# Decoder step: the merge's stick-breaking products placed between the steps of dilated attention

## What is computed

```python
u = rmsnorm(h);  z = u @ W_in        # q, k, v of 12 dilated and 8 stick-breaking heads, gates ga, gb
oa = combine_groups(dilated_prompt(q, k, v, win, dil, slopes) for 3 dilations)   # 256 features a token
ob = sb_prompt(q, k, v, bias)                                                    # 512 features a token

def merge_out(x, oa, ob, ga, gb, w_oa, w_ob, w_out):
    ya = oa.reshape(*lead, H_G * HEAD_DIM) @ w_oa
    yb = ob.reshape(*lead, B_W) @ w_ob
    return x + (jax.nn.sigmoid(ga) * ya + jax.nn.sigmoid(gb) * yb) @ w_out

h += hier_moe(rmsnorm(h))            # one of 4 groups, then 2 of its 8 experts
h += sigmoid(rmsnorm(h) @ w_pg) * (p @ w_pp)
```

## Time and profile before

| | |
|---|---|
| three runs | 1991.63, 1993.75, 1997.38 us (median 1993.75) |
| the profiled execution | 1992.05 us, its span 1990.4 us |
| PE, DVE, ACT, POOL busy over the span | 88%, 60%, 49%, 10% |

### The profile page before, as it was taken

How to read it: one execution, slowest core, us unless ns; L and a number is a source line. 1 busy time by engine, 2 the same in 40 slices (tenths; PEclk the granted TensorE clock), 3 DMA queues, 4 the chain that set the end, 5 groups by cost and what they waited for, 6 DMA issues and landing times. The chain is left out here.

```text
span 1990.4 us, 27436 instructions
## 1 busy us (share of the span) xinstructions
PE 1752.8 (88%) x9832; PEld 1485.7 (75%) x9832; DVE 1201.3 (60%) x1554; ACT 966.8 (49%) x1360; POOL 195.8 (10%) x304
## 2 busy tenths in 40 slices
PE   4999999979888888676688977999999999997498
PEld 3999999978666666454587855788888888885485
DVE  5111222162589997432564246899999999996485
ACT  4221111111566775134442014677777777775255
POOL 1000111130000000000130012111111111110100
PEclk8999999989999999685899978999999999999699
DMA  5443455363351200601336225999999999994641
GB/s 170 108 133 116 128 173 159 117 203 111 119 160 56 73 33 12 201 2 28 120 113 208 100 86 207 390 376 372 376 379 383 368 386 379 377 372 191 222 150 65
DMA packets 154089, 384.28 MB, mean 193 GB/s; under 512 B 21668, under 2 KB 94996, under 8 KB 133525
## 3 DMA queue, kind: packets, MB, share of 16 engines
q1 hardware_dynamic: 119732, 313.43, 44.1%
q0 software_dynamic: 15424, 36.00, 5.6%
q10 hardware_dynamic: 18848, 33.74, 4.8%
HBM read 331.09 MB, written 76.35 MB: 205 GB/s over the span
## 5 line engine op out<-in xcount | busy, mean ns | idle before, releaser
L96 PE MATMUL p_acc<-uh,p_wl 128*128 128x344 f32 x720 | 234.0, 325 | 10.1 <-DVE ul L414 10.1
L97 PE MATMUL p_acc<-ul,p_wh 128*128 128x344 f32 x720 | 230.5, 320 | 0.0
L98 PE MATMUL p_acc<-uh,p_wh 128*128 128x344 f32 x720 | 230.3, 320 | 0.0
L391 ACT ACTIVATE p_zc<-p_acc 128x344 f32<-128x344 f32 x90 | 41.2, 458 | 290.4 <-PE p_acc L98 281.7
L2452 DVE TENSOR_TENSOR x_wgl<-x_wg,x_wgh 128x2048 fp32r<-128x2048 f32 x66 | 148.4, 2288 | 28.0 <-ACT x_wgh L2389 20.3
L2452 DVE TENSOR_TENSOR x_wul<-x_wu,x_wuh 128x2048 fp32r<-128x2048 f32 x66 | 148.3, 2288 | 18.7 <-ACT x_wuh L2389 18.7
L2474 DVE TENSOR_TENSOR x_wdl<-u,x_wdh 128x1024 fp32r<-128x1024 f32 x128 | 148.2, 1220 | 9.7 <-ACT x_wdh L2395 9.7
L96 PEld LDWEIGHTS p_acc<-uh,p_wl 128*128 128x128 f32 x720 | 135.6, 188 | 13.4 <-issue 8.5
L427 DVE COPY u<-p_tp 128x512 f32<-128x512 f32 x40 | 25.8, 686 | 185.3 <-PE p_tp L344 185.3
L97 PEld LDWEIGHTS p_acc<-ul,p_wh 128*128 128x128 f32 x720 | 135.7, 189 | 0.0
L98 PEld LDWEIGHTS p_acc<-uh,p_wh 128*128 128x128 f32 x720 | 135.7, 189 | 0.0
(11 more groups left out here) (378 smaller groups left out, 4240.5 us busy)
## 6 DMA issues: line engine op xcount, KB each, us to landing
x_wg<-in_w_gate SPq DMA_DIRECT2D x64, 1024.0 KB, 7.9
x_wu<-in_w_up SPq DMA_DIRECT2D x64, 1024.0 KB, 7.6
u<-in_w_down SPq DMA_DIRECT2D x32, 2048.0 KB, 12.3
zT<-p_zc ACTq DMA_DIRECT2D x30, 516.0 KB, 2.7
p_w<-in_w_in SPq DMA_DIRECT2D x30, 512.0 KB, 5.4
ztok<-u POOLq DMA_DIRECT2D x20, 512.0 KB, 4.6
m_gate<-gT SPq DMA_DIRECT2D x16, 516.0 KB, 4.4
f_y<-ys POOLq DMA_DIRECT2D x16, 512.0 KB, 5.2
```

What stands on the lines that cost most here:

```text
L96: pe.matmul(out, w_low, m_high, start=first, stop=False)
L97: pe.matmul(out, w_high, m_low, start=False, stop=False)
L98: return pe.matmul(out, w_high, m_high, start=False, stop=last)
L391: act.activation(zc[:, b, s * NS:(s + 1) * NS], acc[b * NSPLIT + s][:, 0:NS], ACT.Copy).then_inc(zc_full, 1)
```

## The change

The 288 products of `w_ob` with the stick-breaking outputs (8 chunks x 3 pieces x 12) leave `merge` and are issued inside `dilated` by `other_part`, by a table `plan`: 12 in each of the steps 15, 16, 17, 36, 37, 56 and 60, and 6 in each of the steps 18 to 35 and 38 to 53. They sum in one bank `yacc`; ACT evicts each piece (`keep`) to `kept_y` and stores a full chunk to DRAM (`ybT`). ACT cuts the high parts (`boh`, `woh`) and GpSimd the low parts (`bol`, `wol`). To find room, q, k and v hold one pair at a time, and SP loads the second pair's over the first's as they come free; the two value banks become one (`O`), its eviction moves to step lag 20, and DVE's eviction to the front of the step. In `merge` a piece has 6 products; `ybT` comes back by DMA with the gates, and is multiplied from SBUF. The constants of `route` are made by GpSimd during `residual`, and ranks and inverse move to before products 0, 4 and 5. mTh, mTl and `x_idx` get longer rows.

```diff
-        EXP_LAG, TURN_LAG, VALUE_LAG, EVICT_LAG, SUM_LAG, INV_LAG, DONE_LAG = 18, 19, 20, 21, 26, 28, 32
+        EXP_LAG, TURN_LAG, VALUE_LAG, EVICT_LAG, SUM_LAG, INV_LAG, DONE_LAG = 18, 19, 20, 20, 26, 28, 32
...
+        M = 3 * CB
+        PIECES = KD * NSPLIT
+
+        first_p1 = score_step(UNITS)
+        plan = {n: M // 2 for n in range(EXP_LAG, first_p1 + UNITS)}
+        plan.update({n: M // 2 for n in range(first_p1 + EXP_LAG, first_p1 + UNITS + EXP_LAG)})
+        plan.update({n: M for n in (EXP_LAG - 3, EXP_LAG - 2, EXP_LAG - 1, first_p1 + EXP_LAG - 2, first_p1 + EXP_LAG - 1,
+                                    first_p1 + UNITS + VALUE_LAG, last_unit[-1] + SUM_LAG - 1)})
+        first_m, n_m = {}, 0
+        for n in sorted(plan):
+            first_m[n] = n_m
+            n_m += plan[n]
+        evict_at = {n + 1: first_m[n] // M for n in plan if (first_m[n] + plan[n]) % M == 0}
+
+        q = sb("q", [P, N_DIL, SEQ])
+        k = sb("k", [P, N_DIL, SEQ])
+        v = sb("v", [P, N_DIL, QT, P])
+        boh = sb("boh", [P, CB, NT], F32R)
+        bol = sb("bol", [P, CB, NT], F32R)
+        woh = sb("woh", [P, 2, CB, P], F32R)
+        wol = sb("wol", [P, 2, CB, P], F32R)
+        wo = g["m_w"][:, :, 2:2 + CB, :]
+        kept_y = g["spare"]
...
-        O = [ps(f"O{n}", [P, 512]) for n in range(2)]
-        nat_ps = O[0][0:ROWS, P:2 * P]
-        inv_ps = O[0][0:ROWS, 2 * P:3 * P]
-        far_ps = O[0][:, 3 * P:3 * P + ROWS].rearrange("p (b i) -> p b i", b=2)
-        sum_ps = O[0][:, 3 * P + ROWS:3 * P + 2 * ROWS].rearrange("p (b i) -> p b i", b=2)
+        O = ps("O", [P, 512])
+        yacc = ps("yacc", [P, 512])
...
+                    if p_ == 0:
+                        sp.wait_ge(row_full, 2 * QT)
+                        load_qk(sp, 1, 0)
+                    else:
+                        sp.wait_ge(o_full, QT)
+                        load_v(sp, 1, [0])
                     sp.wait_ge(row_full, 2 * (p_ + 1) * UNITS)
                     classes_out(p_, mst, 1, mrows[:, p_, 1, :], m_out[p_][1], m_in[p_][1])
+                    if p_ == 0:
+                        load_qk(sp, 1, 1)
+                        load_qk(sp, 1, 2)
+                    else:
+                        sp.wait_ge(o_full, UNITS)
+                        load_v(sp, 1, [1, 2])
...
+            def weight_low(c):
+                pool.wait_ge(woh_full, c + 1)
+                pool.tensor_tensor(wol[:, c % 2, :, :], wo[:, c % 2, :, :], woh[:, c % 2, :, :], ALU.subtract).then_inc(wol_full, 1)
+
+            for c in range(2):
+                weight_low(c)
+            for kk in range(CB):
+                pool.wait_ge(boh_full, kk + 1)
+                pool.tensor_tensor(bol[:, kk, :], obT[:, kk, :], boh[:, kk, :], ALU.subtract).then_inc(bol_full, 1)
+            for c in range(2, KD):
+                weight_low(c)
...
-                if a >= 2:
-                    evicted(a - 2)
-                if a % 2 == 0:
-                    bank_read(at_step)
+                if a >= 1:
+                    evicted(a - 1)
+                bank_read(at_step)
...
+            def other_part(s):
+                for m in range(first_m[s], first_m[s] + plan[s]):
+                    piece, x = divmod(m, M)
+                    c, t = piece // NSPLIT, slice(piece % NSPLIT * NS, (piece % NSPLIT + 1) * NS)
+                    kk, n = divmod(x, 3)
+                    if x == 0:
+                        pe.wait_ge(wol_full, c + 1)
+                        need(pe, y_full, piece)
+                    if piece == 0 and n == 0:
+                        pe.wait_ge(bol_full, kk + 1)
+                    last = pe.matmul(yacc[:, 0:NS], (wol, woh, woh)[n][:, c % 2, kk, :], (boh, bol, boh)[n][:, kk, t],
+                                     start=(x == 0), stop=(x == M - 1), skip_group_check=True)
+                    if x == M - 1:
+                        last.then_inc(yacc_full, 1)
...
+                if s in plan:
+                    other_part(s)
...
+            def load_weight(c):
+                need(act, wol_full, c - 1)
+                act.dma_start(wo[:, c % 2, :, :], wob[:, :, c * P:(c + 1) * P]).then_inc(wo_in[c % 2], 16)
+
+            def weight_high(c):
+                act.wait_ge(wo_in[c % 2], 16 * (c // 2 + 1))
+                need(act, yacc_full, (c - 1) * NSPLIT)
+                act.activation(woh[:, c % 2, :, :], wo[:, c % 2, :, :], ACT.Copy).then_inc(woh_full, 1)
+
+            def keep(piece):
+                c, n = divmod(piece, NSPLIT)
+                need(act, y_out[c % 2], 16 * (c // 2))
+                act.wait_ge(yacc_full, piece + 1)
+                act.activation(kept_y[:, c % 2, n * NS:(n + 1) * NS], yacc[:, 0:NS], ACT.Copy).then_inc(y_full, 1)
+                if n == 0 and 1 <= c and c + 3 < KD:
+                    load_weight(c + 3)
+                if n == NSPLIT - 1:
+                    if c + 2 < KD:
+                        weight_high(c + 2)
+                    act.wait_ge(y_full, piece + 1)
+                    act.dma_start(ybT[c, :, :], kept_y[:, c % 2, :]).then_inc(y_out[c % 2], 16)
...
+            load_v(act, 0, range(N_DIL))
+            for kk in range(CB):
+                act.activation(boh[:, kk, :], obT[:, kk, :], ACT.Copy).then_inc(boh_full, 1)
+            for c in range(2):
+                weight_high(c)
+            for c in range(2, 4):
+                load_weight(c)
+            for c in range(2):
+                act.wait_ge(g["stick_out"][c], 16 * ((2 * KD - DECODE_GATES + 1 - c) // 2))
             for s in range(LAST):
+                if s in evict_at:
+                    keep(evict_at[s])
...
-        KA, KB = 2, CB
-        KO = KA + KB
+        KA = 2
         PASSES = KD // 2
         U = 2 * NSPLIT
-        w = g["m_w"]
-        wh = sb("m_wh", [P, 2, KO, P], F32R)
-        wl = sb("m_wl", [P, 2, KO, P], F32R)
-        oh = sb("m_oh", [P, KO, NT], F32R)
-        ol = sb("m_ol", [P, KO, NT], F32R)
+        w = g["m_w"][:, :, 0:KA, :]
+        wh = sb("m_wh", [P, 2, KA, P], F32R)
+        wl = sb("m_wl", [P, 2, KA, P], F32R)
+        oh = sb("m_oh", [P, KA, NT], F32R)
+        ol = sb("m_ol", [P, KA, NT], F32R)
+        yb = sb("m_yb", [P, 2, NT])
         gate = sb("m_gate", [P, 2, 2, NT])
         part = sb("m_part", [P, 2, 2, NS])
         summed = sb("m_sum", [P, U, NS])
-        bank = [[ctx.enter_context(nc.psum_tensor(f"m_{n}{j}", [P, 512], F32)) for n in ("ya", "yb")]
-                for j in range(3)]
+        bank = [ctx.enter_context(nc.psum_tensor(f"m_ya{j}", [P, 512], F32)) for j in range(3)]
...
+                sp.dma_start(yb[:, b, :], ybT[bass.ds(f, 1), :, :].rearrange("a p n -> (a p) n")).then_inc(g_in[b], 16)
...
-                        for k in range(KO):
+                        for k in range(KA):
                             if isinstance(it, int) and j == 0:
                                 pe.wait_ge(ol_full, k + 1)
-                            last = products(pe, bank[j % 3][k >= KA][:, 0:NS], wh[:, b, k, :], wl[:, b, k, :],
-                                            oh[:, k, t], ol[:, k, t], k in (0, KA), k in (KA - 1, KO - 1))
+                            last = products(pe, bank[j % 3][:, 0:NS], wh[:, b, k, :], wl[:, b, k, :],
+                                            oh[:, k, t], ol[:, k, t], k == 0, k == KA - 1)
...
-                        for x in range(2):
-                            dve.tensor_tensor(part[:, j % 2, x, :], gate[:, b, x, s * NS:(s + 1) * NS],
-                                              bank[j % 3][x][:, 0:NS], ALU.mult).then_inc(part_full, 1)
+                        for x, y in enumerate((bank[j % 3][:, 0:NS], yb[:, b, s * NS:(s + 1) * NS])):
+                            dve.tensor_tensor(part[:, j % 2, x, :], gate[:, b, x, s * NS:(s + 1) * NS], y, ALU.mult)\
+                                .then_inc(part_full, 1)
...
-        BEFORE_RANK, BEFORE_FIRST, BEFORE_SECOND = 2, 7, 8
+        BEFORE_RANK, BEFORE_FIRST, BEFORE_SECOND = 0, 4, 5
...
-            first = {6: ("g", 0), 7: ("g", 1), 8: ("u", 0)}
+            first = {5: ("g", 0), 6: ("g", 1), 7: ("u", 0)}
...
-            dve.wait_ge(const, 12)
+            dve.wait_ge(g["t_const_set"], 12)
...
-            with nc.sbuf_tensor("mTh", [P, KD, NT], F32R) as g["mTh"], nc.sbuf_tensor("mTl", [P, KD, NT], F32R) as g["mTl"]:
+            with nc.sbuf_tensor("mTh", [P, KD, WIDE], F32R) as g["mTh"], nc.sbuf_tensor("mTl", [P, KD, WIDE], F32R) as g["mTl"]:
...
-            g["x_idx"] = held("x_idx", [P, 2, 8], I32)
+            g["x_idx"] = held("x_idx", [P, 2, 16], I32)
```

202 lines of the change are left out of this document (104 added, 98 removed).

## The result

The changed kernel takes 1975.86 us (median of four runs, 1970.39 to 1978.68) against 1994.39 of the kernel before on the same chip (four runs, 1991.63 to 1997.38): a ratio of 0.9909, 95% interval 0.9881 to 0.9938. The profiled execution is 1977.65 us with a span of 1976.0; before, 1992.05 and 1990.4. The forecast was 1976.

What follows compares the result with a forecast made beforehand. TensorE bounds the merge; dilated attention is a ring of TensorE, copies and exp. Dilated -3, merge -17 and routing +3.5 make -16.5 from 1992.05: 1975.5 profiled, 1977.2 median; forecast 1976 us, range 1957 to 1988.

Steps and rivals of the forecast that it cites:

- Steps 20 to 35: Dilated attention, to the end of the last scores: 66.3 us become 59.7 by full clock and shorter VectorE waits, -6.5 us.
- Up to the first exp: Start of dilated attention: 36 moved products, waiting for GpSimd's low parts, delay the first maxima; +4.5 us, bounds 0 and +8.
- Between the pairs: Dilated attention, exchange of maxima: 24 products cost nothing there, the second pair's later v loads cost +1.3 us.
- Second pair: Dilated attention, second pair's values: twelve narrow steps fall from 2.83 to 2.35 us at full clock, wide ones even; -5 us.
- End: End of dilated attention: two lots of 12 products and an eviction, 4.5 us against a 2.83 us DMA wait; +1.8 us.
- Merge: Merge stage: TensorE no longer bounds; VectorE and GpSimd taking turns need 6.5 us a chunk, 61 us against 78.5; -17 us.
- Routing: Routing stage: all nine products now wait for the ranks, and ScalarE ends last, near 1237; +3.5 us, bounds -3 and +5.
- Zero terms: Constants made in the residual stage by idle GpSimd, and longer rows of mTh, mTl and x_idx: 0 us each.
- Half clock: Rival for dilated attention: steps stay at half clock, total near +30 us, 2022 us; chance 0.06.
- ScalarE eating the gain: Rival: ScalarE's extra jobs and the switches make dilated attention +7 instead of -3, total 1986 us; chance 0.2.
- No turns in the merge: Rival: VectorE and GpSimd do not take turns, merge -29 us, total 1964; chance 0.15, or 0.08 for 1958 with faster routing.
- Merge set by the gates' DMA: Rival: the merge stays as it is because the gates' DMA sets it, total 1993 us; chance 0.03.

Runs made afterwards that it cites:

- few_products: Changed kernel issuing only the last of every twelve moved products (24 of 288), merge values wrong; 1974.35 us in one run, steps 63.6 us instead of 54.8.
- weights_late: Changed kernel with ScalarE's first two w_ob loads issued behind its loads of v; first values at 41.8 us, against 41.5.
- low_parts_first: Changed kernel with GpSimd making the four low parts of the stick-breaking outputs ahead of the first two weights'; first values at 37.2 us instead of 41.5.
- merge_bank: Changed kernel whose second gate product reads the first's PSUM bank instead of the SBUF tile, values wrong; 1965.34 us in one run, merge 61.7 instead of 64.4.
- route_back: Changed kernel with ranks, inverses and first expert's weight cuts put back to their old positions in routing; 1972.63 us, ratio 0.9898 to the kernel before.

## Why the prediction was right, point by point

**The total** was right to 0.2 us of the median, and that close a hit is luck. The four runs spread over 8 us. My own sum gave 1975.5 for the profiled execution and 1977.2 for the median, and I wrote 1976 without saying why. And errors cancelled: dilated attention was 1.5 us better and the merge 3.1 us worse than forecast, and inside dilated attention the steps were 5 us better and the gap between the pairs 3.8 us worse.

**Steps 20 to 35** (-6.5, measured -11.5). The two causes named were right, the clock (8.8 us by few_products) and the wide steps' wait for VectorE (in the 2.7 us left), also the choice of the row at 700 to 750 us for the clock. The mis-sized term is the step: "1.9 of old work + 1.15" counts the drain of the transposes twice, once in the old step and once as a switch; the next product starts 0.41 us after the last group of transposes starts (its row says 0.66). Measured 2.75 instead of 3.0 narrow, 5.11 instead of 5.3 wide, and 3.2 us for the last step where I had 4.3. That ScalarE's extra jobs fit was right.

**Up to the first exp** (+4.5, measured +5.8 for `far_maxima`, +6.3 for the values). Durations of the cuts were near (0.98, 0.57, 2.37 and 1.26 us for the estimated 1.05, 0.6, 2.4 and 1.3), and that the clock could fall to half was named. What was mis-sized is GpSimd's end, 829.0 and so 30.4 us into the stage, where I had 29.3, and the clock: the products behind piece 0 took 7.1 us, inside my 4.5 to 8 but over its middle, 3.4 us of them at half clock. What stands behind `far_maxima` cost 0.5 us, where I had 0.8. That q and k came 1.5 us later behind the two weight loads, where I had allowed only for a lighter DMA load ("bounds 0"), is true but did not set the first values, as weights_late shows. What I did not ask is why GpSimd should start with the weights: low_parts_first shows what that order cost.

**Between the pairs** (+1.3, measured +5.1): the worst term. The exchange came 8.7 us after the last scores instead of 5.9, and the rest is v, which was named and mis-sized (2.15 us of wait); and "24 products lie in the exchange, at nothing" was true of the products. But each third piece issues a store of 516 KB, and I costed that DMA at nothing; with a weight's load beside it, it stretched the exchange by 2 us (8.8 to 6.7 once both were moved). Counting the DMAs of the moved steps, and not only their products, would have found it.

**Second pair** (-5, measured -6.7): the steps at full clock are 2.1 to 2.2 us, forecast 2.35 (twelve of which are 28.2 us, not the 28.5 that I wrote). The first ones, behind the wait for v, were still at half clock. **End**: +2.3 for +1.8.

**Merge** (-17, measured -13.9). The turns were right and are shown twice, by the stretched products and by their cure. The first products came 8.3 us into the stage (forecast 9), but chunks take 7.0 us on average and 7.4 in the ring shown, not 6.5, and the reason is the one I had put at the bound ("where the loads come late"): "two chunks ahead they come just in time" forgot that the load of a buffer begins only when its products have ended, which closes a ring through load, sigmoid and cuts. Busy DMA share, 0.60, hides this: the ring waits for latency.

**Routing** (+3.5, measured +2.7, and +2.4 by the mean of the ten profiles with the new positions). The steps came as forecast: ranks at 14.0 us into the stage (14.5), products from 16.4 (17), ScalarE last, 55.1 us (55). The rows of the changed kernel, which starts this stage at 1165.94:

```profile
1179.94 1.33 PE L2195 MATMUL t_rank_ps<-t_both,t_tri 128*128 128x288 f32 x2 [4.37 <-DVE t_both L2241]
...
1182.31 0.78 PE L97 MATMUL t_pp<-t_wpph,t_pTl 128*128 128x512 f32 x1
...
1219.11 1.91 ACT L2134 ACTIVATE x_wuh<-x_wu 128x2048 fp32r<-128x2048 f32 x1 [0.37 <-ACT u L2128]
...
1223.18 1.97 PE L2406 MATMUL x_tpx<-ident,x_x 128*128 128x128 f32 x8 [7.11 <-PEq L2021]
```

**Zero terms.** Longer rows: the residual stage takes 138.8 to 140.1 us, mean 139.4, in the twelve profiles that have them and the constants in it, 138.8 before; a price of up to a microsecond for either is neither shown nor excluded, and neither was tried by itself.

**Rivals.** Half clock: out by the windows. ScalarE eating the gain: out, the steps have no waits left. No turns in the merge: out by merge_bank. Merge set by the gates' DMA: half true, as a member of the ring.

## What to carry to other kernels

Work moved into the gaps of a stage that waits can cost that stage next to nothing, if the stage otherwise stands at TensorE's lower clock: ask of every stretch at a granted clock of 0.5 what could fill it, before asking how to shorten it. Charge a moved step with its DMAs as well, and look for small transfers on a critical exchange that share the engines with them. With double buffers, add up the ring (issue, landing, each engine's part, release) and not only the busiest member; an order of two loops on an idle engine, with the clock that went with it, was worth as much here as the whole stage's forecast gain.

## What the hardware did that I had not expected

- TensorE's clock stayed at 0.50 for 26.5 us of few_products (829.5 to 856) though the engine was busy 23.2 of them, and rose on its own at about 856 with the same kind of step.
- A short wait ahead of the first values goes with a fall of the clock in some profiles and not in others: 3.4 us at half clock in the changed kernel, none in route_back, whose dilated attention has the same code.
- Beside GpSimd's addition, a VectorE product of 344 columns takes 0.50 us with one operand in PSUM and 1.07 with both in SBUF; GpSimd's own 0.92 us does not change with it.
- Two small transfers had landed 5.25 us after their issue beside a 516 KB store and a weight load, 3.23 without them but behind the loads of v; in the kernel before it was 2.62 (899.53 to 902.15).
